# Fourteen full-precision products as pairs of fp32r products, and the order of the query stage, in a two-layer decoder step

## The chip, the cores and the metric

One core of a Trainium2 chip runs the whole step as one program. The metric is the device time of one execution in microseconds (us). The kernel before took 736.26 us (median of 3 runs, 736.24 to 736.81). 0.2% of it is 1.5 us.

## What is computed

A step of a decoder trunk with two layers, for 256 prompt tokens and 8 new tokens of running sequences; the kernel treats the 264 together, as columns of matrices whose rows are features. Cut to what matters here:

```python
def rmsnorm(x, g):
    y = xf * rsqrt(mean(xf * xf, axis=-1) + EPS)      # over the features of a token
    return y * g

# layer 0: norm, gated token MLP, residual; norm "ffn0", SwiGLU, residual
# keys:    c, kr = latent and rotary part of rmsnorm(h) @ w_dkv; c normed ("lat"), kr through rope
# layer 1: norm "mix1"; cq = rmsnorm(hn @ w_dq)  ("q"); q = cq @ w_uq   (16 heads x (128 + 64))
#          q_rope = rope(q_rope); attention over latents; residual; norm "ffn1", SwiGLU, residual
# final norm

def rope(x, pos):
    x1, x2 = split(x, 2, axis=-1)
    return concatenate([x1 * cos - x2 * sin, x2 * cos + x1 * sin], axis=-1)
```

All inputs and outputs are fp32.

## The kernel before

**Products.** A weight product in fp32 quality is made of three fp32r products (fp32r is the reduced form of fp32 that TensorE takes at a higher rate): each operand is split into a rounded high part and the rest, and `passes` (L1371) adds high by high, high by low and low by high in PSUM. The moving operand always has 264 columns (T), the stationary one is a 128x128 block. Weights come in slabs of eight blocks (512 KB): SyncE issues the load, ScalarE (ACT) rounds (`whi`, L480), GpSimd subtracts (`wlo`, L414), TensorE (PE) uses them; four slabs are in flight. Activations are rounded by ACT and subtracted by VectorE (DVE, `lo_of`, L836).

**Norm sums.** Per norm, ACT squares a tile of h (L485), DVE adds it to `acc`, which lies in PSUM bank 5; the last addition writes `total` in SBUF (L851). `norm_sum` (L1394) multiplies a 128x128 matrix of ones by `total` in plain fp32 into bank 4, after the first chunk of the next stage. ACT takes the reciprocal root (`root`), DVE refines it in three steps (`inverse_root`). Eight norms: mix0, v, ffn0, mix1, q, lat, ffn1, final.

**Rope.** Rows of two heads' rotary parts lie in 128 partitions. Their halves are exchanged by a product with a permutation matrix `swap`. DVE multiplies the query rows by sine (`tt`) and by cosine (`sq`), PE exchanges the sine part in plain fp32 (`query_swap`, L1611), DVE adds the cosine part in PSUM (`query_turned`). ACT rounds the result into `qrb` (`turned_queries`), DVE writes its low part beside it (`query_turned_low`). The rotary keys go the same way, once, through bank 5 (L1632).

**The stage "qa"** is the place of most of the change. Eight pairs of heads; per pair three chunks of nine products: chunk 0 into bank 0 (rotary parts), chunks 1 and 2 into banks 1 and 2 (the heads' other parts). Every engine works through an order written out by hand, with semaphores between them. There is one bank for each of the three chunks, so a chunk of pair p+1 can start only when DVE has read that of pair p: bank 0 when sine and cosine products are done (`rope_cos`, L1590), banks 1 and 2 when the heads' low parts are done (`qlow_done`). Turned queries lie in bank 3 (even pairs) and bank 5 (odd pairs). Bank 5 is also that of the turned keys: the first odd exchange waits for their low part (`krlo_done`, L1616).

```python
            queries(1)                         # PE, L1633
            for p in range(2, PAIRS, 2):
                query_swap(p - 2)
                query_swap(p - 1)
                queries(p)
                queries(p + 1)
```

So two exchanges stand together ahead of two pairs of chunks. DVE does two pairs per turn as well: it adds both turned queries, then takes the next pair's sine and cosine, low parts of turned queries and of heads in alternation. ACT rounds the heads (L722, L723), splits slabs between them (L480), and does the turned queries of two pairs together ahead of them. An activation table is loaded behind the queries of pair 1 (L492). The latents are scaled on DVE in pairs 2 and 3 and copied wide on ACT (L740, L743) in pairs 4 and 5. After the stage come the keys of the first pair, the sample queries (L1720) and the first scores (L1680).

Of the kernel before, what the change touches and what calls it, by code (L numbers as in the profile page):

```python
# [89 lines left out]
def build(nc, xT, w_stream, w_uv, gains, v_gain, lat_gain, q_gain, wsT, ws00_in, bs, cosT, sinT, w_ukT, pages, table,  # L90
          y_out, c_out, kr_out, v_out):
    with ExitStack() as ctx:
# [16 lines left out]
        ones = sb("ones", [P, P])  # L109
# [69 lines left out]
        swap = work[:, 6, 0:P]  # L179
# [34 lines left out]
        def room(p, n):  # L214
# [34 lines left out]
            sem, ("sq_done", "acc_done", "sum_done", "root_done", "norm_step", "rms_ready"))  # L249
        xhi_done, xlo_done = map(sem, ("xhi_done", "xlo_done"))  # L250
# [9 lines left out]
        swap_done, cqr_done, lat_done, cqs_done, cqhi_done, cqlo_done, krs_done, krsin_done, krswap_done, krsum_done, kr_done, krhi_done, krlo_done = map(  # L260
            sem, ("swap_done", "cqr_done", "lat_done", "cqs_done", "cqhi_done", "cqlo_done", "krs_done", "krsin_done", "krswap_done", "krsum_done", "kr_done", "krhi_done",
# [4 lines left out]
        q_done, qnhi_done, qlow_done, rope_cos, rope_sin, rope_swap, qr_done, qrhi_done, qrlo_done = map(  # L266
            sem, ("q_done", "qnhi_done", "qlow_done", "rope_cos", "rope_sin", "rope_swap", "qr_done", "qrhi_done", "qrlo_done"))
# [141 lines left out]
        def _(pool):  # L409
# [15 lines left out]
            pool.memset(ones[:], 1.0).then_inc(const_done, 1)  # L425
# [26 lines left out]
            for z in range(4):  # L452
                pool.tensor_copy(swap[:, 32 * z:32 * z + 32], ident[:, 32 * (z ^ 1):32 * (z ^ 1) + 32]).then_inc(swap_done, 1)
# [19 lines left out]
        def _(act):  # L473
# [29 lines left out]
            def prepare(name, m, i=0, k=0):  # L503

                at = i * k + m if k else m
                square(NQ[name], m, h[:, at, :], i, k)
                if name != "final":
                    gained(name, at)
# [4 lines left out]
            def gained(name, at):  # L513
                act.activation(xhi[:, at, :], h[:, at, :], ACT.Copy,
                               scale=gn[:, G[name], at, :]).then_inc(xhi_done, 1)
                if name == "mix1":
# [168 lines left out]
            for d in range(KQ):  # L685
                split(s0 + d + AHEAD)
                act.wait_ge(cqr_done, d + 1)
                square(NQ["q"], d, ps[:, d, 0:T])

# [12 lines left out]
            split(s0 + 2 + AHEAD)  # L702

# [25 lines left out]
            act.wait_ge(krsum_done, 1)  # L729
            act.activation(krhi, ps[:, 5, 0:NP_], ACT.Copy).then_inc(krhi_done, 1)  # L730
            act.activation(kr[:], ps[:, 5, 0:T], ACT.Copy).then_inc(kr_done, 1)
# [53 lines left out]
            turned_queries(PAIRS - 2)  # L785
# [49 lines left out]
        def _(dve):  # L835
# [4 lines left out]
            def add_square(q, m, i=0, k=0):  # L840
# [10 lines left out]
                dve.tensor_tensor(total[:] if last else acc, acc, sq[:, m % 2, :], ALU.add).then_inc(acc_done, 1)  # L851
# [29 lines left out]
            def gained(name, m, at, i=0, k=0):  # L881
                per = 2 if name == "mix1" else 1
                for z, (gain, hi, lo) in enumerate(((name, xhi, xlo), ("kv", x2hi, x2lo))[:per]):
# [3 lines left out]
                                             op1=ALU.subtract).then_inc(xlo_done, 1)  # L887

# [189 lines left out]
            for d in range(KQ):  # L1078
                dve.wait_ge(slab_used, s0 + d + 1)
                dve.tensor_tensor(ps[:, d, 0:T], ps[:, d, 0:T], Ra[:], ALU.mult).then_inc(cqr_done, 1)  # L1080
                add_square(NQ["q"], d)

# [34 lines left out]
            dve.tensor_tensor(kp, kp, Ra, ALU.mult).then_inc(krs_done, 1)  # L1117
            dve.wait_ge(krs_done, 1)
            dve.wait_ge(cqlo_done, KQ)
            dve.tensor_tensor(Ra, kp, sinb, ALU.mult).then_inc(krsin_done, 1)  # L1120
            dve.tensor_tensor(tt[:, 0, :], kp, cosb, ALU.mult).then_inc(psum_read, KQ + 3)

            def keys_turned():

                dve.wait_ge(krswap_done, 1)
                dve.wait_ge(psum_read, QA_N)
                dve.tensor_tensor(ps[:, 5, 0:T], ps[:, 5, 0:T], tt[:, 0, :], ALU.add).then_inc(krsum_done, 1)

            def keys_turned_low():
# [3 lines left out]
                dve.wait_ge(krhi_done, 1)  # L1133
# [14 lines left out]
            def query_rope(p):  # L1148
# [11 lines left out]

            def query_turned(p):

                dve.wait_ge(rope_cos, p + 1)
                dve.wait_ge(rope_swap, p + 1)
                dve.tensor_tensor(turned_bank(p), turned_bank(p), sq[:, p % 2, :], ALU.add).then_inc(qr_done, 1)
# [11 lines left out]
            keys_turned()  # L1177
            inverse_root("lat", Rc)
            keys_turned_low()
            query_rope(1)  # L1180
            query_low(1, 0)
            query_low(1, 1)
            for g in range(1, PAIRS // 2):
                query_turned(2 * g - 2)
                query_turned(2 * g - 1)
                query_rope(2 * g)
                query_turned_low(2 * g - 2)
                query_low(2 * g, 0)
                query_turned_low(2 * g - 1)
                query_low(2 * g, 1)  # L1190
                if g == 1:
                    latents(0)
                query_rope(2 * g + 1)
# [812 lines left out]
```

## Time and profile before

| | before |
|---|---|
| median of 3 runs | 736.26 us |
| profiled execution | 736.79 us |
| its span, first to last instruction | 735.1 us |
| PE busy | 725.5 us, 99% |
| ACT busy | 408.4 us, 56% |
| DVE busy | 306.8 us, 42% |
| GpSimd (POOL) busy | 534.9 us, 73% |
| granted clock of PE, mean | 0.998 |

The page and the trace come from one execution, the profiled one; 1.7 us of it lie outside the span. Busy is the time in which an engine ran at least one instruction; PE's weight loads (PEld) run beside its products. Times in time lines count from the start of the span. The profile records a plain fp32 product as two instructions, and the ends of matmuls are modelled, so that the distance between two starts says more than a duration.

### The profile page before, as it was taken

The numbers are of one execution on the slowest core, as the hardware profiler recorded it, in microseconds if no ns is written. First come the engines' busy times: TensorE is split into PE (matmuls) and PEld (weight loads), VectorE is DVE, ScalarE is ACT, GpSimd is POOL, SyncE is SP. The second block draws the span as 40 slices with busy tenths as digits, with TensorE's granted clock in tenths as the row PEclk, the third lists the DMA queues.
The fourth block names the chain that finished last, engine by engine and source line by source line (L and its number), as shares of the span: only waits on it lengthen the run. The fifth ranks groups of instructions, "written<-read, shape, count | busy, mean of one in ns | idle before, by whom it ended". The sixth has DMA issues, their size and how long they took to land.

```text
span 735.1 us, 16687 instructions
## 1 busy us (share of the span) xinstructions
PE 725.5 (99%) x6255; PEld 709.1 (96%) x6255; DVE 306.8 (42%) x777; ACT 408.4 (56%) x743; POOL 534.9 (73%) x252
## 2 busy tenths in 40 slices
PE   9999999999999999999999999999999999999995
PEld 8999999999999999999999888799999999999995
DVE  5446986233333222232488766753233333221002
ACT  7877555455444444555677576665554444444542
POOL 4895778869878888889868122149878878888891
PEclk9999999999999999999999999999999999999999
DMA  7864455656777755566576898326546555556641
GB/s 260 260 207 139 134 169 176 201 173 211 241 238 231 235 186 173 199 200 203 174 255 192 263 386 310 134 68 218 174 148 198 183 186 180 191 171 197 203 146 60
DMA packets 44842, 144.68 MB, mean 197 GB/s; under 512 B 5650, under 2 KB 6674, under 8 KB 44530
## 3 DMA queue, kind: packets, MB, share of 16 engines
q1 hardware_dynamic: 44498, 143.50, 59.3%
q8 instruction: 36, 0.59, 0.3%
q0 software_dynamic: 144, 0.40, 0.1%
q14 instruction: 20, 0.16, 0.1%
q10 hardware_dynamic: 144, 0.02, 0.0%
HBM read 142.42 MB, written 1.48 MB: 196 GB/s over the span
## 4 chain that ended last, share of the span: by engine, by line
PE 95%; DVE 2%; ACT 1%; DMA 1%; issue 0%; SPq 0%; DVEq 0%; ACTq 0%
PE ps L1373 29%; PE ps L1374 29%; PE ps L1375 29%; PE ps L1774 1%; PE ps L1750 1%; PE ps L1694 1%; DMA h<-xT 1%; PE ps L1503 1%; PE ps L1621 0%; PE ps L1754 0%; PE ps L1412 0%; PE ps L1680 0%; ACT whi L480 0%; DVE ps L851 0%; PE ps L1682 0%
## 5 line engine op out<-in xcount | busy, mean ns | idle before, releaser
L414 POOL TENSOR_TENSOR wlo<-raw,whi 128x1024 fp32r<-128x1024 f32 x221 | 527.1, 2409 | 182.5 <-ACT whi L480 182.4
L1373 PE MATMUL ps<-xhi,whi 128*128 128x264 f32 x1000 | 286.9, 287 | 0.0
L1374 PE MATMUL ps<-xlo,whi 128*128 128x264 f32 x1000 | 283.3, 283 | 0.0
L1375 PE MATMUL ps<-xhi,wlo 128*128 128x264 f32 x1000 | 283.2, 283 | 0.0
L480 ACT ACTIVATE whi<-raw 128x1024 fp32r<-128x1024 f32 x221 | 232.7, 1054 | 50.5 <-PE ps L1375 48.3
L1374 PEld LDWEIGHTS ps<-xlo,whi 128*128 128x128 f32 x1000 | 188.5, 189 | 0.2
L1373 PEld LDWEIGHTS ps<-xhi,whi 128*128 128x128 f32 x1000 | 188.3, 188 | 0.3
L1375 PEld LDWEIGHTS ps<-xhi,wlo 128*128 128x128 f32 x1000 | 187.6, 188 | 0.0
L1373 PE MATMUL ps<-ahi,whi 128*128 128x264 f32 x352 | 100.0, 284 | 0.0
L1375 PE MATMUL ps<-ahi,wlo 128*128 128x264 f32 x352 | 99.9, 284 | 0.0
L1374 PE MATMUL ps<-alo,whi 128*128 128x264 f32 x352 | 99.9, 284 | 0.0
L1035 DVE TENSOR_TENSOR h<-ps,h 128x264 f32<-128x264 f32 x31 | 13.4, 433 | 142.3 <-PE ps L1375 142.3
L1375 PEld LDWEIGHTS ps<-ahi,wlo 128*128 128x128 f32 x352 | 66.3, 188 | 0.0
L1374 PEld LDWEIGHTS ps<-alo,whi 128*128 128x128 f32 x352 | 66.2, 188 | 0.0
L1373 PEld LDWEIGHTS ps<-ahi,whi 128*128 128x128 f32 x352 | 66.2, 188 | 0.0
L664 ACT ACTIVATE ahi<-ps 128x264 f32 (+1 forms) x44 | 17.2, 392 | 87.2 <-DVE ps L1054 87.2
L1051 DVE TENSOR_TENSOR ps<-ps,work 128x264 f32<-128x264 f32 x44 | 19.4, 442 | 104.4 <-PE ps L1375 104.4
L485 ACT ACTIVATE sq<-h 128x264 f32<-128x264 f32 x39 | 16.3, 423 | 51.8 <-DVE h L1035 51.4
L661 ACT ACTIVATE sq<-ps 128x264 f32<-128x264 f32 x44 | 17.2, 392 | 41.2 <-DVE ps L1049 41.2
L1373 PE MATMUL ps<-ohi,whi 128*128 128x264 f32 x128 | 36.5, 285 | 0.0
L1373 PE MATMUL ps<-ghi,whi 128*128 128x264 f32 x128 | 36.4, 284 | 0.0
L1374 PE MATMUL ps<-glo,whi 128*128 128x264 f32 x128 | 36.3, 283 | 0.0
(266 smaller groups left out, 1148.8 us busy)
## 6 DMA issues: line engine op xcount, KB each, us to landing
raw<-w_stream SPq DMA_DIRECT2D x221, 512.0 KB, 3.4
pg<-pages SPq DMA_DIRECT2D x64, 288.0 KB, 4.5
pg<-w_ukT SPq DMA_DIRECT2D x1, 2048.0 KB, 9.3
pg<-w_uv SPq DMA_DIRECT2D x1, 2048.0 KB, 10.0
h<-xT SPq DMA_DIRECT2D x4, 264.0 KB, 4.7
raw<-w_stream SPq DMA_DIRECT2D x4, 256.0 KB, 5.5
y_out<-raw SPq DMA_DIRECT2D x4, 198.0 KB, 2.3
wsraw<-wsT SPq DMA_DIRECT2D x1, 512.0 KB, 5.6
```

Of the source, the lines that this page charges most:

```text
L414: pool.tensor_tensor(wlo[:, c % RING, :], raw[:, c % RING, :], whi[:, c % RING, :].bitcast(F32), ALU.subtract).then_inc(lo_ready, 1)
L480: act.activation(whi[:, c % RING, :], raw[:, c % RING, :], ACT.Copy).then_inc(hi_ready, 1)
L485: act.activation(sq[:, m % 2, :], src, ACT.Square).then_inc(sq_done, 1)
L661: act.activation(sq[:, w % 2, :], ps[:, (n0 + 2 * w) % BANKS, 0:T], ACT.Silu).then_inc(silu_done, 1)
L664: act.activation(ahi[:, i * 2 + w, :], ps[:, (n0 + 2 * w + 1) % BANKS, 0:T], ACT.Copy).then_inc(ahi_done, 1)
L1035: dve.tensor_tensor(h[:, at, :], ps[:, bank, 0:T], h[:, at, :], ALU.add).then_inc(psum_read, 1)
L1051: dve.tensor_tensor(up, up, Ra[:], ALU.mult).then_inc(usc_done, 1)
L1373: pe.matmul(out, whi_, mhi, start=start, stop=False)
L1374: pe.matmul(out, whi_, mlo, start=False, stop=False)
L1375: return pe.matmul(out, wlo_, mhi, start=False, stop=stop)
L1503: pe.matmul(both, vthi[:, at, c, :], wsboth[:, c, g], start=True, stop=False)
L1694: last = pe.transpose(ps[:, 2 + e, b * P:b * P + P], pr[:, e, b * P:b * P + P], ident[:])
```

## The change

1. Sums: for ffn0, mix1, q, lat and ffn1 the last addition stays in `acc` (PSUM). ACT writes its rounded part `total_hi`, DVE the rest `total_lo`, and `norm_sum` is two fp32r products with the same ones. mix0, v and final stay as they were.
2. Exchanges: rows are rounded and exchanged first, and multiplied by the sine afterwards. ACT writes `rhi` from bank 0, DVE the cosine product and the rest `rlo`; PE exchanges both in fp32r (`swap_r`); DVE multiplies by sine in place and subtracts from the cosine part. Bank 0 is free after `rlo` and the cosine product. The keys go the same way (`kphi`, `kplo`).
3. Order: PE does the exchange of pair p-1 behind chunk 0 of pair p. DVE and ACT go pair by pair. The two ACT copies of the turned keys move between the heads of pair 1. On DVE the low part of a head that frees a bank stands ahead of the low parts of turned queries, and the steps of the lat root and the low part of the keys come behind the rope products of pair 1 and the first turned queries.

```diff
+            def total_high(name):                                   # ACT
+                q = NQ[name]
+                act.wait_ge(acc_done, ACC0[q] + NORMS[q][2])
+                act.wait_ge(sum_done, q)
+                act.activation(total_hi[:], acc, ACT.Copy).then_inc(total_hi_done, 1)
...
             def queries(p, done):                                   # ACT
+                wait_query(act, 3 * p)
+                if p > 1:
+                    act.wait_ge(rope_swap, p - 1)
+                act.activation(rhi[:, p % 2, :], ps[:, 0, 0:T], ACT.Copy).then_inc(rope_hi, 1)
                 for e in range(2):
                     x = 3 * p + 1 + e
+                    if e and p == 1:
+                        act.wait_ge(krsum_done, 1)
+                        act.activation(krhi, ps[:, 5, 0:NP_], ACT.Copy).then_inc(krhi_done, 1)
+                        act.activation(kr[:], ps[:, 5, 0:T], ACT.Copy).then_inc(kr_done, 1)
...
             done = queries(1, done)
             table(ACT.Exp)
-            for g in range(1, PAIRS // 2):
-                turned_queries(2 * g - 2)
-                turned_queries(2 * g - 1)
-                done = queries(2 * g, done)
-                if g == 2:
+            turned_queries(0)
+            for p in range(2, PAIRS):
+                done = queries(p, done)
+                turned_queries(p - 1)
+                if p == 4:
                     act.wait_ge(c_done, KL)
                     act.activation(cThi[:], ps[:, 6:8, 0:NP_], ACT.Copy).then_inc(cthi_done, 1)
-                done = queries(2 * g + 1, done)
-                if g == 2:
+                if p == 5:
                     act.activation(cT[:], ps[:, 6:8, 0:T], ACT.Copy).then_inc(ct_done, 1)
...
+            def total_low(name):                                    # DVE
...
+                lo_of(total_lo[:], acc, total_hi[:]).then_inc(total_lo_done, 1)
...
-                dve.tensor_tensor(tt[:, 1 + p % 2, :], ps[:, 0, 0:T], sinb, ALU.mult).then_inc(rope_sin, 1)
+                dve.wait_ge(rope_hi, p + 1)
                 dve.tensor_tensor(sq[:, p % 2, :], ps[:, 0, 0:T], cosb, ALU.mult).then_inc(rope_cos, 1)
+                lo_of(rlo[:, p % 2, :], ps[:, 0, 0:T], rhi[:, p % 2, :]).then_inc(rope_lo, 1)
...
-            keys_turned()
-            inverse_root("lat", Rc)
-            keys_turned_low()
-            query_rope(1)
-            query_low(1, 0)
-            query_low(1, 1)
-            for g in range(1, PAIRS // 2):
-                query_turned(2 * g - 2)
-                query_turned(2 * g - 1)
-                query_rope(2 * g)
-                query_turned_low(2 * g - 2)
-                query_low(2 * g, 0)
-                query_turned_low(2 * g - 1)
-                query_low(2 * g, 1)
...
+            for p in range(1, PAIRS):
+                query_rope(p)
+                if p == 1:
+                    keys_turned()
+                query_sine(p - 1)
+                query_low(p, 0)
+                query_turned(p - 1)
+                if p == 1:
+                    inverse_root("lat", Rc)
+                    keys_turned_low()
+                query_low(p, 1)
+                query_turned_low(p - 1)
+                if p in (2, 3):
+                    latents(p - 2)
...
-            for p in (PAIRS - 2, PAIRS - 1):
-                query_turned(p)
-            query_turned_low(PAIRS - 2)
+            query_sine(PAIRS - 1)
+            query_turned(PAIRS - 1)
...
+                n = SPLIT_SUMS.index(name) + 1                      # PE, norm_sum
+                pe.wait_ge(total_hi_done, n)
+                pe.matmul(ps[:, 4, 0:T], ones_r[:], total_hi[:], start=True, stop=False)
+                pe.wait_ge(total_lo_done, n)
+                pe.matmul(ps[:, 4, 0:T], ones_r[:], total_lo[:], start=False, stop=True).then_inc(sum_done, 1)
...
-                pe.matmul(turned_bank(p), swap, tt[:, 1 + p % 2, :], start=True, stop=True).then_inc(rope_swap, 1)
+                pe.matmul(turned_bank(p), swap_r[:], rhi[:, p % 2, :], start=True, stop=False)
+                pe.matmul(turned_bank(p), swap_r[:], rlo[:, p % 2, :], start=False, stop=True).then_inc(rope_swap, 1)

             def queries(p):
                 for z in range(3):
                     query_chunk(p, z)
+                    if p and z == 0:
+                        query_swap(p - 1)
```

The exchange of pair 1 still waits for `krlo_done`. `total_high` stands on ACT right behind the last xhi of a stage (for q and lat behind the last square, and for lat behind a split), `total_low` on DVE behind the last xlo.

## Rows read from the trace of the kernel before

**Rows 1.** The page: busy us, share of the span, instructions.

```profile
PE 725.5 (99%) x6255; PEld 709.1 (96%) x6255; DVE 306.8 (42%) x777; ACT 408.4 (56%) x743; POOL 534.9 (73%) x252
```

**Rows 2.** The page: the chain that ended last, by engine.

```profile
PE 95%; DVE 2%; ACT 1%; DMA 1%; issue 0%; SPq 0%; DVEq 0%; ACTq 0%
```

**Rows 3.** Groups by form, PE: form and count, then busy us, mean ns, idle us.

```profile
L1374 PEld LDWEIGHTS ps<-xlo,whi 128*128 128x128 f32 x1000 | 188.5, 189 | 0.2
...
L1621 PE MATMUL ps<-tt,work 128*128 128x264 f32 x16 | 4.2, 386 | 0.0
...
L1399 PE MATMUL ps<-work,ones 128*128 128x264 f32 x12 | 3.6, 384 | 0.0
```

**Rows 4.** Time line, PE, at the lat sum: start us, us, what.

```profile
373.40 0.61 PE L1399 MATMUL ps<-work,ones 128*128 128x264 f32 x2
373.85 0.61 PE L1632 MATMUL ps<-work 128*128 128x264 f32 x2
...
374.42 0.28 PE L1374 MATMUL ps<-xlo,whi 128*128 128x264 f32 x1
```

**Rows 5.** Time line, PE, exchanges of pairs 0 and 1, and chunk 2.0.

```profile
377.56 1.05 PE L1621 MATMUL ps<-tt,work 128*128 128x264 f32 x4
...
378.57 0.28 PE L1374 MATMUL ps<-xlo,whi 128*128 128x264 f32 x1
...
379.66 0.28 PE L1374 MATMUL ps<-xlo,whi 128*128 128x264 f32 x1
```

**Rows 6.** Time line, ACT, stage "qa".

```profile
377.01 1.06 ACT L480 ACTIVATE whi<-raw 128x1024 fp32r<-128x1024 f32 x1
...
378.02 0.41 ACT L723 ACTIVATE ohi<-ps 128x264 fp32r<-128x264 f32 x1
378.44 1.28 ACT L492 ACT_TABLE_LOAD   x1
...
379.84 0.16 ACT L712 ACTIVATE work<-ps 128x8 f32<-128x8 f32 x1
...
380.70 0.18 ACT L712 ACTIVATE work<-ps 128x8 f32<-128x8 f32 x1
...
390.76 0.60 ACT L740 ACTIVATE cThi<-ps 128x512 fp32r<-128x512 f32 x1
```

**Rows 7.** Time line, DVE, stage "qa"; brackets: idle before, and who ended it.

```profile
375.93 0.43 DVE L867 SCALAR_TENSOR_TENSOR work<-ps,work 128x264 f32<-128x264 f32 x1
376.40 0.42 DVE L838 TENSOR_TENSOR krboth<-ps,krboth 128x256 fp32r<-128x256 f32 x1
376.74 0.42 DVE L1154 TENSOR_TENSOR tt<-ps,work 128x264 f32<-128x264 f32 x1
...
378.46 0.43 DVE L838 TENSOR_TENSOR olo<-ps,ohi 128x264 fp32r<-128x264 f32 x1 [0.61 <-ACT ohi L723]
...
379.74 0.43 DVE L1154 TENSOR_TENSOR tt<-ps,work 128x264 f32<-128x264 f32 x1 [0.16 <-PE ps L1375]
...
382.52 0.88 DVE L838 TENSOR_TENSOR qrb<-ps,qrb 64x256 fp32r<-64x256 f32 x2
383.43 0.43 DVE L838 TENSOR_TENSOR olo<-ps,ohi 128x264 fp32r<-128x264 f32 x1
383.78 0.49 DVE L1139 SCALAR_TENSOR_TENSOR ps<-ps,gl,work 128x264 f32<-128x264 f32 x1
```

**Rows 8.** Time line, PE and DVE, from the stage's end to the first scores.

```profile
402.32 1.91 PE L1720 MATMUL ps<-pg,qns 128*8 128x256 f32 x32
404.17 0.39 PE L1680 MATMUL ps<-xhi,ohi 128*128 128x256 f32 x1
...
403.14 0.69 DVE L838 TENSOR_TENSOR xhi<-ps,xhi 128x512 fp32r<-128x512 f32 x1
```

**Rows 9.** Time line, DVE and PE, around the mix1 sum.

```profile
352.98 0.43 DVE L851 TENSOR_TENSOR work<-ps,sq 128x264 f32<-128x264 f32 x1 [0.49 <-ACT sq L485]
...
354.75 0.61 PE L1399 MATMUL ps<-work,ones 128*128 128x264 f32 x2
```

More of the change, by code:

```diff
@@ L178, in build @@
         krhi, krlo = krboth[:, 0], krboth[:, 1]
-        swap = work[:, 6, 0:P]
+        swap_r = sb("swap_r", [P, P], F32R)
+        rhi, rlo = xhi[:, 4:6, :], xlo[:, 4:6, :]
+        kphi, kplo = xhi[:, 6, :], xlo[:, 6, :]
+        total_hi = sb("total_hi", [P, T], F32R)
+        total_lo = sb("total_lo", [P, T], F32R)
+        SPLIT_SUMS = ("ffn0", "mix1", "q", "lat", "ffn1")
         halves = lambda x: x.rearrange("p (a k) -> p a k", a=2)
@@ L702, in _ @@
             split(s0 + 2 + AHEAD)
+            total_high("lat")
+            act.wait_ge(krs_done, 1)
+            act.activation(kphi, ps[:, 3, 0:T], ACT.Copy).then_inc(krhi_done, 1)
             def splits_up_to(c, done):
@@ L850, in add_square @@
                     wait(dve, sum_done, q)
-                dve.tensor_tensor(total[:] if last else acc, acc, sq[:, m % 2, :], ALU.add).then_inc(acc_done, 1)
+                whole = last and not any(q == NQ[name] for name in SPLIT_SUMS)
+                dve.tensor_tensor(total[:] if whole else acc, acc, sq[:, m % 2, :], ALU.add).then_inc(acc_done, 1)
+            def total_low(name):
+                q = NQ[name]
+                dve.wait_ge(acc_done, ACC0[q] + NORMS[q][2])
+                dve.wait_ge(total_hi_done, SPLIT_SUMS.index(name) + 1)
+                dve.wait_ge(sum_done, q)
+                lo_of(total_lo[:], acc, total_hi[:]).then_inc(total_lo_done, 1)
             def inverse_root(name, R):
@@ L887, in gained @@
                                              op1=ALU.subtract).then_inc(xlo_done, 1)
+                    if z == 0 and m == KD - 1 and name in SPLIT_SUMS:
+                        total_low(name)
             dve.memset(ps[:, 5:8, T:512], 0.0).then_inc(zero_done, 1)
@@ L1398, in norm_sum @@
                 pe.wait_ge(acc_done, ACC0[q] + NORMS[q][2])
-                pe.matmul(ps[:, 4, 0:T], ones[:], total[:], start=True, stop=True).then_inc(sum_done, 1)
+                if name not in SPLIT_SUMS:
+                    pe.matmul(ps[:, 4, 0:T], ones, total[:], start=True, stop=True).then_inc(sum_done, 1)
+                    return
+                n = SPLIT_SUMS.index(name) + 1
[3 more added lines that the diff above has]
+                pe.matmul(ps[:, 4, 0:T], ones_r[:], total_lo[:], start=False, stop=True).then_inc(sum_done, 1)
             x_of = lambda b: (xhi[:, b, :], xlo[:, b, :])
@@ L1417, in busy @@
                 for _ in range(times):
-                    pe.matmul(ps[:, 3, 0:P], ones[:], ones[:], start=True, stop=True)
+                    pe.matmul(ps[:, 3, 0:P], ones, ones, start=True, stop=True)
             pe.wait_ge(const_done, 1)
@@ L1512, in _ @@
             pe.wait_ge(acc_done, ACC0[q] + KS)
-            pe.matmul(ps[:, 4, 0:NS], ones[:], total[:, NP_:T], start=True, stop=True)
+            pe.matmul(ps[:, 4, 0:NS], ones, total[:, NP_:T], start=True, stop=True)
             for c in range(2):
@@ L1611, in query_swap @@
             def query_swap(p):
-                pe.wait_ge(rope_sin, p + 1)
+                pe.wait_ge(rope_hi, p + 1)
+                pe.wait_ge(rope_lo, p + 1)
+                pe.wait_ge(swap_done, 4)
                 if p == 0:
@@ L1629, in _ @@
             norm_sum("lat")
-            pe.wait_ge(krsin_done, 1)
-            pe.wait_ge(swap_done, 4)
-            pe.matmul(ps[:, 5, 0:T], swap, Ra, start=True, stop=True).then_inc(krswap_done, 1)
-            queries(1)
-            for p in range(2, PAIRS, 2):
-                query_swap(p - 2)
-                query_swap(p - 1)
+            pe.wait_ge(krhi_done, 1)
+            pe.wait_ge(psum_read, QA_N)
+            pe.matmul(ps[:, 5, 0:T], swap_r[:], kphi, start=True, stop=False)
+            pe.matmul(ps[:, 5, 0:T], swap_r[:], kplo, start=False, stop=True).then_inc(krswap_done, 1)
+            for p in range(1, PAIRS):
                 queries(p)
-                queries(p + 1)
-            query_swap(PAIRS - 2)
             query_swap(PAIRS - 1)
@@ L1907, in _ @@
             for z in range(2):
-                pe.matmul(ps[:, SUM_BANKS[z], half[z]], ones[:], total[:, half[z]], start=True, stop=False)
+                pe.matmul(ps[:, SUM_BANKS[z], half[z]], ones, total[:, half[z]], start=True, stop=False)
             for z in range(2):
                 pe.wait_ge(sql_done, z + 1)
-                pe.matmul(ps[:, SUM_BANKS[z], half[z]], ones[:], sq[:, (KD - 1) % 2, half[z]], start=False,
+                pe.matmul(ps[:, SUM_BANKS[z], half[z]], ones, sq[:, (KD - 1) % 2, half[z]], start=False,
                           stop=True).then_inc(suml_done, 1)
```

61 lines of the change are left out of this document (32 added, 29 removed).

## The prediction

> **What bounds the kernel now.** I read the busy shares first: TensorE (PE) is busy for 99% of the span [rows 1]. The chain of work that ended last agrees: 95% of it is PE, and no other engine or queue has more than 2% [rows 2]. So PE time taken out of any stage comes off the end, as long as nobody makes PE wait in its place. The groups by form then show what the change aims at: a full-precision fp32 product is recorded as two passes, twelve for the six 264-column norm sums and sixteen for the eight query exchanges [rows 3]. Last I read the time lines of the stage "qa" (the queries), since there the change also re-orders ACT and DVE. One caution: this trace shows PE as busy whenever a modelled matmul end reaches the next start, so a wait of some tenths does not appear as idle time; start-to-start times are what to read.
>
> **What the products save.** From the start of a norm sum to the next fp32 product is 0.45 us (373.40 to 373.85). The key exchange then ends one product before 374.42: at 374.30, again 0.45 us [rows 4]. Two query exchanges run from 377.56 to 378.45 (one product before 378.57), 0.445 each. A nine-product chunk of queries runs from 378.57 to 379.66, 1.09 us or 0.121 us per fp32r product [rows 5]. Two fp32r products cost 0.24 us, so each replaced product saves 0.205 us. Eight query exchanges, one key exchange and five sums are fourteen: 2.9 us less PE work. No row shows an fp32r product right beside one of another form; bounds: 1.9 us if one of each two costs its operand's load (0.19 us [rows 3]) instead of 0.12, 3.0 us if the replaced product is taken at 0.45 and rounded up. I take 2.9, since the same fp32r form with 264 columns runs 0.121 us apart throughout [rows 5].
>
> The Trainium skill ("FP8 and Floating Point Precision", its list of precision modes) counts true fp32 as four passes, high by high down to low by low. The trace has two records per product and 0.445 against 0.121 us, 3.7 times; with four passes' worth the gain would be 14 x (4 - 2) x 0.121 = 3.4 us, an estimate by that page. The measured 0.205 stands.
>
> **The five sums.** Each gets one ACT copy (0.3 to 0.4 us) and one DVE subtraction (0.43) ahead of it, after the last addition of squares. PE works a whole chunk between the two. The tightest is mix1: the addition begins at 352.98 and ends at 353.41, the sum starts at 354.75 [rows 9]. Copy and subtraction are done by about 354.4, and the low product comes 0.12 us after the high one; the rows of xlo that PE needs earlier are written ahead of both. For "q" ACT has a split of a slab (0.95) put behind the new copy, and GpSimd has that slab to split only several us before PE wants it. Cost nothing, bounds 0 to 0.3 us each if a split slips; I take 0. POOL's and SP's queues are not changed; POOL waits longer for cT, below.
>
> **The stage of the queries.** Here the cover must be worked out. Names: chunk p.0 is the nine products of pair p's rotary queries into bank 0, p.1 and p.2 those of its heads. Before, PE needed for bank 0 only two DVE products (sine, cosine), with no ACT work ahead. Now ACT must first round (rhi), then DVE does cosine and low part: bank 0 hangs on ACT's queue. Per pair PE drops to 3 x 1.09 + 0.24 = 3.5 us, while ACT gets about 0.3 more and DVE one product more. The step times that I use, start to start: DVE product 0.34 (376.40 to 376.74), 0.47 when it waits for the one before (375.93 to 376.40), the two low halves of turned queries 0.91 (382.52 to 383.43), one latent 0.4 (0.49 long, less the tenth by which the others overlap); PE's end to DVE or ACT 0.2 (from 379.54, one product before 379.66, to 379.74); ACT's start to a DVE subtraction of its result 0.44 (378.02 to 378.46) [rows 5 to 7]. On ACT a split and the small copy behind it take 1.0 (377.01 to 378.02), ohi and table load up to the turned queries' first copy 1.82 (378.02 to 379.84), turned queries 0.86 (379.84 to 380.70), rhi or any other copy 0.28 [rows 6]. All clock times now are those of the trace before, savings of the three sums ahead left out.
>
> Pair 1. The lat sum starts at 373.40, the key exchange follows at 373.64, chunk 1.0 at 373.88 (was 374.30). It ends 374.97; rhi 375.17; DVE cosine 375.60, low part 375.95. Then DVE goes on in its order: two products for the keys (376.29, 376.76), sine 0 (377.10), a head's low part (377.45), turned 0 (377.8), three steps of the lat root (378.1, 378.6, 379.1), and only then the keys' low half, 379.55 to 380.0. PE has chunks 1.0 to 1.2 and 2.0 done at 378.46 and stands at the exchange of pair 1, whose bank 5 the keys' low half must free: **wait 1.5 us**. In the kernel before, the low half was at 376.40, ahead of all queries of pair 1.
>
> Independently, ACT is late: split 376.83, two key copies until 378.34, ohi 378.41, table load, turned 0 at 380.23, rhi 2 at 381.09; DVE has the low halves of turned 0 until 381.63, cosine 381.63, low part done at 382.46. Chunk 3.0 would come at 380.9 without the wait above and comes at 382.43 with it: the same 1.5 us again, and not in addition. So two chains bind here.
>
> Pair 3 and on. ACT from 381.09: copy, heads and two splits (0.28 + 0.17 wait + 2 x 1.3), turned 1 at 384.1, rhi 3 at 384.97. DVE: low halves of turned 1 from 384.6, latent, so cosine 3 at 385.9 and low part done at 386.75; PE is there at 385.95: **wait 0.8**. The same recurrence, with a split behind the second head of pairs 3 and 4, the wide copies of cT (0.6 us [rows 6]) ahead of rhi 5 and rhi 6, and the wide low part ahead of pair 7's cosine, gives 0.2 at chunk 5.0, 0.5 at 6.0, 0.2 at 7.0, 0.3 at the last exchange. At the hand-over, DVE takes low halves 6, sine 7 and turned 7 before the first keys' low part (0.7 us, formerly begun at 403.14): done at 406.0, PE there at 405.55 after keys and the sample queries, which took 1.85 us (402.32 to 404.17) [rows 8]: **wait 0.45**. POOL gets cT three us later than before, and has the first keys' slab split still before PE comes to it.
>
> Sum of waits: 1.5 + 0 + 0.8 + 0.2 + 0.5 + 0.2 + 0.3 + 0.5 = 4.0 us. Bounds: 1.0 us if ACT and DVE catch up wherever chains do not bind twice, 6 us if each of eight stops also costs a tenth or two of restart. Net +1.1 us. In the profiled execution: 736.8 (span 735.1 and 1.7 around it) becomes 737.9; its time is 0.5 above the median of the runs, so on the median 736.26 becomes 737.3 us.
>
> For the table load the Trainium skill ("ScalarE: Activation LUTs", What ACT_TABLE_LOAD costs) gives about 1.28 us and as much again of drain, 2.66 in all. The trace shows 1.28 and the next ACT instruction at once: 1.40 us from 378.44 to 379.84 [rows 6]. With the page's drain rhi 2 would come 1.3 us later and the sum would be +2.4; the row decides.
>
> **Rivals.** (A) Forecast, 0.48: PE's saved time is given back in waits in "qa", 736.3 to 738.3. (B) The covers hold, 0.13: waits of 0.5 us in all; 736.3 - 2.9 + 0.5 = 733.9. For it speaks that ACT and DVE have idle time in the stage; against it that ACT's work from the first split of pair 1 up to rhi 3 has only 0.2 us of idle time in my count. (C) Only the keys' low half waits, 0.15: 2.9 saved, 1.5 given back, 734.9. For it: it is the longest wait and comes from DVE's written order alone; against: the later loop needs ACT to gain 0.3 us per pair. (D) Slower, 0.24: the restart. When PE has stood, the load of the stationary operand (0.19 us [rows 3]) and the semaphore are no longer hidden behind running products; eight stops at 0.2 add 1.6: 738.9. It decides from about 0.06 us per stop on; for it speaks that rows show such a load under every product, against it that loads might go ahead of the wait.
>
> **How the numbers follow.** 0.2% is 1.5 us, what a measurement can tell here; so faster means under 734.8, slower over 737.7. Faster: B and a third of C, 0.17. Slower: D and a fifth of A, 0.33. Same: 0.50. The likeliest is A, 737.3 us, its own range 736.3 to 738.3. The range takes in C and most of D: 734.8 to 739.0; B is what is left out.
>
> **What would show it.** After: sums and exchanges 0.24 us from start to start; PE's start at the exchange of pair 1 some 1.5 us behind the end of chunk 2.0; ACT without gaps between pairs 1 and 4; rhi later than 0.2 us behind the end of chunk p.0 from pair 2 on; first scores about 1.8 us later, counted from chunk 0.0. I am wrong if the turned keys' low half is done before chunk 2.0 ends, or if chunk 4.0 follows 3.2 without a gap.

## The result, and the profile after

| | before | changed |
|---|---|---|
| median | 736.25 us | 737.57 us (737.25 to 738.03) |
| ratio, 95% interval | | 1.0019 (1.0012 to 1.0026) |
| profiled execution | 736.79 us | 737.78 us |
| its span | 735.1 us | 736.0 us |

The changed kernel is 1.3 us slower (0.9 to 1.9 by the interval), against 1.1 forecast. Each median is of 16 executions; one of those before took 1838 us, which does not move the median. The mean granted clock of PE is 0.998 in both profiled executions. The page of the changed kernel, busy us by engine and then the chain that ended last, answers to [rows 1, 2]:

```profile
PE 724.4 (98%) x6255; PEld 708.2 (96%) x6255; DVE 311.0 (42%) x791; ACT 413.1 (56%) x757; POOL 534.4 (73%) x252
...
PE 90%; DVE 5%; ACT 3%; issue 1%; DMA 1%; SPq 0%; DVEq 0%; ACTq 0%
```

PE has less work, and its share of the chain fell from 95% to 90%; DVE and ACT, 2% and 1% before, have 5% and 3%. The groups by form of the changed kernel (busy us, mean ns, idle us before) answer to [rows 3]:

```profile
L1668 PE MATMUL ps<-xhi,swap_r 128*128 128x264 f32 x8 | 2.4, 304 | 1.7 <-DVE krboth L862 1.6
L1669 PE MATMUL ps<-xlo,swap_r 128*128 128x264 f32 x8 | 2.3, 284 | 0.0
...
L1441 PE MATMUL ps<-total_hi,ones 128*128 128x264 f32 x5 | 1.4, 285 | 0.0
L1443 PE MATMUL ps<-total_lo,ones 128*128 128x264 f32 x5 | 1.4, 283 | 0.0
```

The new products are there: two fp32r products in place of each fp32 one (the profile calls the memory of `rhi` and `rlo` xhi and xlo). Whom PE waited for, by line, in the changed kernel (us in total, times, longest):

```profile
PE ps L1668 <- DVE krboth L862: 1.6, 1, 1.6
PE ps L1462 <- POOL one L434: 1.1, 1, 1.1
PE ps L1410 <- DVE xlo L862: 1.0, 2, 0.6
...
PE ps L1726 <- DVE xhi L862: 0.3, 1, 0.3
```

The wait for POOL's `one` was there before, in the first microseconds. The three rows for DVE are new, and all their waits lie between the lat sum and the first scores. PE's time line there (start us, us, what), answering to [rows 4, 5, 8]:

```profile
372.58 0.29 PE L1441 MATMUL ps<-total_hi,ones 128*128 128x264 f32 x1
372.70 0.28 PE L1443 MATMUL ps<-total_lo,ones 128*128 128x264 f32 x1
372.83 0.29 PE L1682 MATMUL ps<-xhi,swap_r 128*128 128x264 f32 x1
...
373.07 0.29 PE L1410 MATMUL ps<-xhi,whi 128*128 128x264 f32 x1
...
377.55 0.28 PE L1412 MATMUL ps<-xhi,wlo 128*128 128x264 f32 x1
379.46 0.36 PE L1668 MATMUL ps<-xhi,swap_r 128*128 128x264 f32 x1 [1.64 <-DVE krboth L862]
379.66 0.28 PE L1669 MATMUL ps<-xlo,swap_r 128*128 128x264 f32 x1
...
386.24 0.39 PE L1410 MATMUL ps<-xhi,whi 128*128 128x264 f32 x1 [0.60 <-DVE xlo L862]
386.47 0.29 PE L1411 MATMUL ps<-xlo,whi 128*128 128x264 f32 x1
...
405.69 0.36 PE L1726 MATMUL ps<-xhi,ohi 128*128 128x256 f32 x1 [0.32 <-DVE xhi L862]
```

Sum and key exchange take 0.24 to 0.25 us each (372.58 to 372.83 to 373.07). After chunk 2.0 PE stands from 377.67 (one product after 377.55) to 379.46. Who holds it is seen on DVE's time line of the changed kernel:

```profile
378.31 0.43 DVE L900 SCALAR_TENSOR_TENSOR work<-ps,work 128x264 f32<-128x264 f32 x1
378.78 0.42 DVE L862 TENSOR_TENSOR krboth<-ps,krboth 128x256 fp32r<-128x256 f32 x1
...
384.11 0.87 DVE L862 TENSOR_TENSOR qrb<-ps,qrb 64x256 fp32r<-64x256 f32 x2 [0.82 <-ACT qrb L736]
385.02 0.50 DVE L1178 SCALAR_TENSOR_TENSOR ps<-ps,gl,work 128x264 f32<-128x264 f32 x1
...
385.77 0.42 DVE L862 TENSOR_TENSOR xlo<-ps,xhi 128x264 fp32r<-128x264 f32 x1
```

The keys' low half (krboth) is written behind the root's last step and ends at 379.20. For chunk 4.0 PE waits until the low part of pair 3 ends at 386.19; that is late because DVE stood 0.82 us for ACT's turned queries, which stand behind two splits. ACT's time line of the changed kernel:

```profile
378.02 1.28 ACT L500 ACT_TABLE_LOAD   x1
...
379.42 0.16 ACT L733 ACTIVATE work<-ps 128x8 f32<-128x8 f32 x1
379.48 0.77 ACT L736 ACTIVATE qrb<-ps 64x256 fp32r<-64x256 f32 x2
...
382.70 1.08 ACT L488 ACTIVATE whi<-raw 128x1024 fp32r<-128x1024 f32 x1
...
383.70 0.79 ACT L736 ACTIVATE qrb<-ps 64x256 fp32r<-64x256 f32 x2
384.51 0.39 ACT L743 ACTIVATE xhi<-ps 128x264 fp32r<-128x264 f32 x1
```

The executions differ at their start, ahead of every edit, by up to 1.4 us (the first norm's sum starts at 16.91 us in e3 and at 18.28 us in e1), and a little at their end, so I compare stages, by PE's starts: from the lat sum to the first scores, and from there to the second half of the final norm's sum. The first norm's sum is at 17.52 us before and at 17.26 in the changed kernel. All in us; the last column is the median's distance from the kernel before, from the ratio.

| kernel | lat sum | scores | stage | rest | against before |
|---|---|---|---|---|---|
| before | 373.40 | 404.17 | 30.77 | 322.77 | |
| changed | 372.58 | 405.69 | 33.11 | 322.78 | +1.4 |
| e1_sums_only | 373.53 | 404.07 | 30.54 | 322.59 | -1.3 |
| e10_exchanges_only | 372.75 | 406.41 | 33.66 | 322.98 | +2.7 |
| e2_keys_first | 372.73 | 404.72 | 31.99 | 322.79 | +0.5 |
| e3_table_late | 372.67 | 405.78 | 33.11 | 322.78 | +1.7 |
| e4_both | 372.56 | 403.77 | 31.21 | 322.77 | -0.4 |
| e5_splits_alone | 372.75 | 404.81 | 32.06 | 322.78 | +0.4 |
| e6_splits | 373.58 | 404.96 | 31.38 | 322.78 | -0.3 |
| e7_between | 372.44 | 404.53 | 32.09 | 322.78 | 0.0 |
| e8_best | 372.63 | 404.40 | 31.77 | 323.69 | +1.0 |
| e9_ordered | 373.49 | 403.30 | 29.81 | 324.81 | +0.4 |
| e11_ordered_splits | 372.26 | 402.15 | 29.89 | 322.75 | -1.8 |
| e12_second_order | 372.58 | 401.57 | 28.99 | 322.80 | -2.4 |

The stage lost 2.34 us though ten of the fourteen replaced products lie in it.

### The profile page after: what moved, and what is told of

It reads as the page before. It is cut to its first block, busy times and chain, and to the rows that moved or that the text cites. A ratio compares the mean times of both kernels' runs of the same rounds, so it can differ in the third digit from the quotient of the medians.

```text
span 736.0 us, 16754 instructions
## 1 busy us (share of the span) xinstructions
PE 724.4 (98%) x6255; PEld 708.2 (96%) x6255; DVE 311.0 (42%) x791; ACT 413.1 (56%) x757; POOL 534.4 (73%) x252
## 4 chain that ended last, share of the span: by engine, by line
PE 90%; DVE 5%; ACT 3%; issue 1%; DMA 1%; SPq 0%; DVEq 0%; ACTq 0%
PE ps L1410 28%; PE ps L1411 28%; PE ps L1412 27%; PE ps L1820 1%; PE ps L1796 1%; DMA h<-xT 1%; PE ps L1740 1%; ACT whi L488 1%; PE ps L1547 1%; PE ps L1456 0%; DVE qrb L862 0%; PE ps L1800 0%; ACT tt L783 0%; PE ps L1726 0%; DVE ps L876 0%
```

## The experiments

My theory: the products save what was computed (0.205 us each), the sums cost nothing, and all that is lost is waits in the stage of the queries, from two chains: DVE's order (keys' low half late) and ACT's queue (table load, splits ahead of `rhi`). Rivals: the sums hide a cost; only one of the chains binds; restarts are what costs.

**e1_sums_only.** The sums as changed, exchanges and orders as before. Against the kernel before:

```diff
+        SPLIT_SUMS = ("ffn0", "mix1", "q", "lat", "ffn1")
...
+                pe.matmul(ps[:, 4, 0:T], ones_r[:], total_hi[:], start=True, stop=False)
...
+                pe.matmul(ps[:, 4, 0:T], ones_r[:], total_lo[:], start=False, stop=True).then_inc(sum_done, 1)
```

> The kernel before with the five sums alone as pairs of fp32r products; exchanges and order as before. Theory (products are worth 0.205 us each and ACT and DVE have room around the sums): 5 x 0.205 = 1.0 us less than before, 735.2 us; sums 0.24 us from start to start, no wait of PE at any of them. Rival (the copies ahead of the sums make PE wait, or a saved product is given back elsewhere): no change, or slower than before.

Measured: 735.09 us, 0.9982 (0.9972 to 0.9991): -1.3 us where five times 0.205 is 1.0. The stage is 0.23 shorter, one sum's worth, and so is the rest (0.18). So the sums' copies cost nothing that shows here.

**e10_exchanges_only.** The other half of the change: the changed kernel with plain fp32 sums.

```diff
-        SPLIT_SUMS = ("ffn0", "mix1", "q", "lat", "ffn1")
+        SPLIT_SUMS = ()
```

> The changed kernel with the five sums as plain fp32 products again. Theory (the sums' saving adds to whatever the query stage does): 1.0 us more than the changed kernel, 738.6 us; same waits of PE in the stage of the queries. Rival (the sums' copies ahead of that stage push ACT late and cause part of the waits): less than 0.5 us more, or even less time than the changed kernel.

Measured: 738.88 us, 1.0036 (1.0022 to 1.0049), 1.3 us above the changed kernel by the ratios. With e1 this splits the change: the sums bring 1.3, exchanges and order cost 2.7, together +1.4, which is the change. The same waits were expected, and they are not quite the same: the stage is 0.55 us longer than in the changed kernel where the lat sum accounts for 0.2. The other 0.35 is at chunk 6.0, where PE loses 1.04 us from start to start instead of 0.70. Why was not tried.

**e2_keys_first.** The keys' chain alone: ACT rounds the turned keys ahead of pair 1's first head, DVE adds them ahead of pair 1 and takes their low half before the head's.

```diff
-                    if e and p == 1:
+                    if e == 0 and p == 1:                       # ACT: krhi, kr
...
+            keys_turned()                                       # DVE
             for p in range(1, PAIRS):
                 query_rope(p)
                 query_sine(p - 1)
+                if p == 1:
+                    keys_turned_low()                           # was behind inverse_root
```

> The changed kernel, with the turned keys and their low half ahead on DVE (turned keys before pair 1, low half right behind sine 0) and the two key copies on ACT ahead of the heads of pair 1. Theory (two chains bind at the same place, the second is ACT's: two key copies, table load, turned queries 0, then rhi 2): the wait at the exchange of pair 1 (1.87 us lost in the changed kernel) goes, but chunk 3.0 then waits about 1 us for rhi 2, and only what ACT gained by its key copies standing earlier stays: 0.5 to 0.6 us less than the changed kernel. Rival (the keys' low half alone costs the time): 1.9 us less.

Measured: 736.78 us, 1.0007 (0.9998 to 1.0016), 0.9 under the changed kernel, where theory had 0.5 to 0.6 and the rival 1.9. Whom PE waited for in e2_keys_first:

```profile
PE ps L1410 <- DVE xlo L862: 1.5, 3, 0.8
```

and where, on its time line:

```profile
381.21 0.39 PE L1410 MATMUL ps<-xhi,whi 128*128 128x264 f32 x1 [0.82 <-DVE xlo L862]
```

The wait at the exchange of pair 1 is gone, and 0.82 us stand at chunk 3.0, where there was none: the second chain, as the theory has it. From start to start it is 1.08 us where 1.87 stood. Much of the difference is that ACT's table load came 0.56 earlier, counted from the lat sum (377.61 - 372.73 against 378.02 - 372.58), with the key copies moved. Chunk 4.0 lost 0.3 less as well (0.58 against 0.87).

**e3_table_late, e4_both.** The table load moved behind the stage, alone and together with e2's edit.

```diff
             done = queries(1, done)
-            table(ACT.Exp)
...
             act.activation(qlt[:, 0:2, :], key_views(6), ACT.Copy).then_inc(qla_done, 1)
+            table(ACT.Exp)
```

> The changed kernel with the table load for Exp taken out of the queries' stage and put behind the copy of the sample queries, where ACT waits for PE anyway. Theory (the exchange of pair 1 binds first and ACT then waits for chunk 2.1): same as the changed kernel within 0.3 us, with 1.3 us more idle time on ACT ahead of rhi 2. Rival (ACT's queue alone sets the stage): 1.4 us less.

> Both edits, keys first and table load late. Theory (both chains had to go): 1.8 us less than the changed kernel, 735.8 us, more than the sum of the two alone (0.5 and 0); the wait at the exchange of pair 1 is gone, that at chunk 3.0 is some 0.3 us, and those at chunks 4.0 and later stay. Rival (effects add up): 0.6 us less.

Measured: e3 738.3 us, 1.0023 (1.0014 to 1.0033), no gain; e4 735.9 us, 0.9995 (0.9986 to 1.0004), 1.8 under the changed kernel. PE in e3_table_late:

```profile
379.55 0.36 PE L1668 MATMUL ps<-xhi,swap_r 128*128 128x264 f32 x1 [1.63 <-DVE krboth L862]
```

and in e4_both:

```profile
380.48 0.39 PE L1410 MATMUL ps<-xhi,whi 128*128 128x264 f32 x1 [0.24 <-DVE xlo L862]
```

1.3 us of ACT work taken out brings nothing while the keys' chain holds PE. Of the stage, e3 takes 0.0, e2 1.1 and both 1.9: two chains side by side.

**e5_splits_alone, e6_splits.** A slab's split comes right behind `rhi` instead of behind a head (one split of pair 4 stays behind its first head), so that turned queries and the next `rhi` don't wait for it; e5 on the changed kernel, e6 on e4.

```diff
                 act.activation(rhi[:, p % 2, :], ps[:, 0, 0:T], ACT.Copy).then_inc(rope_hi, 1)
+                done = splits_up_to(min(QA_S + KQ * (3 * p + 1) // BLK + AHEAD + 1, PR_S + AHEAD), done)
                 for e in range(2):
...
-                    done = splits_up_to(min(QA_S + KQ * x // BLK + AHEAD + 1, PR_S + AHEAD), done)
```

> The changed kernel with one edit on ACT: the slabs' splits stand right behind rhi, ahead of the heads, instead of behind each head (one of pair 4 behind its first head). Same work, same queues otherwise. Theory (from chunk 4.0 on bank 0 is late because rhi stands behind a split and the turned queries): the 1.87 us at the exchange of pair 1 stay, those at chunks 4.0, 5.0, 6.0 (0.87, 0.09, 0.70) go for the most part: 1.3 to 1.7 us less than the changed kernel, 736.1 us. Rival (DVE's own order is what makes chunks 4.0 and 6.0 late): within 0.3 us of the changed kernel.

> All three edits: keys first, table load late, splits behind rhi. Theory: left of the waits are those of the last exchange and the hand-over (0.3 and 0.4 us) and some tenths; 1.2 us less than with the first two edits alone, 734.7 us. Rival: an earlier split makes PE wait for a weight slab or GpSimd late; no gain over the first two edits.

Measured: e5 736.89 us, 1.0005 (0.9996 to 1.0014), 1.0 under the changed kernel and short of what I expected. From start to start, the waits at chunks 4.0 and 5.0 are gone and that at 6.0 is 0.4 shorter, but those at 7.0 and the last exchange are 0.16 longer each. e6 736.18 us, 0.9996 (0.9987 to 1.0005): nothing beyond e4, where 1.2 us were expected. PE in e6_splits:

```profile
381.97 0.39 PE L1412 MATMUL ps<-xhi,whi 128*128 128x264 f32 x1 [0.36 <-DVE xlo L864]
```

Measured from start to start as in the table of the waits below, chunks 4.0, 5.0 and 6.0 lose 0.7 us less than in e4, but chunk 2.2, which lost nothing, now loses 0.36, and chunk 3.0 (this line, 0.63 against 0.51), chunk 7.0 and the last exchange lose 0.4 more together. Moving one piece in ACT's queue moved the waits.

**e7_between.** On e6: turned queries taken between the heads of the next pair, on ACT and on DVE.

```diff
                 for e in range(2):
+                    if e and p:
+                        turned_queries(p - 1)                   # ACT
...
-                query_low(p, 0)                                 # DVE
                 query_turned(p - 1)
+                query_low(p, 0)
...
-                query_low(p, 1)
                 query_turned_low(p - 1)
+                query_low(p, 1)
```

> As the run with the three edits, and the turned queries of pair p-1 on ACT between the two heads of pair p, on DVE ahead of the heads' low halves. Theory (rhi then comes 0.2 us behind the end of chunk p.0 in every pair): 0.2 to 0.5 us less than the three edits, every chunk p.0 follows without a gap. Rival (the second head becomes late and chunk p.2 waits in its place): same or slower than the three edits.

Measured: 736.63 us, 1.0000 (0.9991 to 1.0009); the rival named the place. PE's wait in e7_between:

```profile
380.02 0.39 PE L1412 MATMUL ps<-xhi,whi 128*128 128x264 f32 x1 [1.00 <-DVE olo L864]
```

and the work that it stood for, on DVE:

```profile
378.63 0.88 DVE L864 TENSOR_TENSOR qrb<-ps,qrb 64x256 fp32r<-64x256 f32 x2
379.54 0.43 DVE L864 TENSOR_TENSOR olo<-ps,ohi 128x264 fp32r<-128x264 f32 x1
```

So the order of the low halves matters, which the changed kernel has the other way round: here 0.9 us of turned queries' low halves stand ahead of a head's low part and hold bank 2, and PE with it at chunk 2.2.

**e8_best.** On e7: the first keys' low part ahead of pair 7's sine product and addition.

```diff
+            keys_low(0)
             query_sine(PAIRS - 1)
             query_turned(PAIRS - 1)
-            keys_low(0)
```

> As the run before it, with the first keys' low half on DVE ahead of sine 7 and turned 7. Theory: the 0.36 us lost ahead of the first scores go; in all about 2.9 us minus 0.3 of waits less than the kernel before, 733.8 us, faster than both kernels. Rival: the sample queries become late behind it (their copy on DVE is delayed) and the gain is nil.

Measured: 737.4 us, 1.0013 (1.0004 to 1.0022), 1.0 above e7, where 733.8 us had been expected; the rival named the sample queries. The stage is 0.3 shorter, but the rest 0.9 longer. PE in e8_best, after the first scores:

```profile
406.94 1.06 PE L1778 MATMUL ps<-ident,work 128*128 128x128 f32 x8 [0.39 <-DVE work L1253]
```

The scores have their operand earlier, and the sample queries, which need pair 7 whole, have theirs later.

**e9_ordered, e11_ordered_splits, e12_second_order.** So many places trade with each other that single moves don't find the end. From the start-to-start times of the traces I reckoned whole orders for ACT, DVE and PE, written as lists. They keep e4's edits (keys early, table late) and put the last exchange behind the first keys. e11 has e9's orders but for two splits; e12's lists differ throughout. The edit from e9 to e11, and the start of e12's list for DVE (lo: `rlo`; low: a head's low part; tlow: turned queries' low halves; trn: their addition; inv: the root's steps; kmul, ksub, krlo: turned keys):

```diff
-   "... ohi.6.0 ohi.6.1 rhi.7 tq.5 ohi.7.0 tq.6 ohi.7.1 split.10 khi tq.7 split.11"    # ACT, e9
+   "... ohi.6.0 ohi.6.1 split.10 rhi.7 tq.5 ohi.7.0 split.11 tq.6 ohi.7.1 khi tq.7"    # ACT, e11
...
+   "mem cos.0 lo.0 low.0.0 kmul inv.1 low.0.1 ksub sine.0 inv.2 trn.0 cos.1 lo.1 inv.3 krlo low.1.0
+    low.1.1 sine.1 trn.1 cos.2 lo.2 low.2.0 tlow.0 low.2.1 tlow.1 cos.3 lo.3 sine.2 ..."  # DVE, e12
```

> All fourteen products as pairs of fp32r products, with a new order of ACT, DVE and PE in the stage of the queries, laid out from the start-to-start times of the traces so that no engine makes PE wait: rhi never behind a split and turned queries together, one split per pair between the heads, the keys' low half ahead of exchange 1, exchanges of some pairs after chunk 1 or 2, the table load behind the sample queries, the first keys' low half ahead of the last turned low halves. Same work on every engine. Theory (the change loses by the order alone): from the lat sum to the first scores 28.5 to 29.5 us (30.8 before, 33.1 in the changed kernel); 2.0 to 3.0 us faster than before, 733.3 to 734.4 us. Rival (ACT and DVE have no room for the added work in any order): 31 us or more between those marks, no faster than before.

> The ordered kernel with the last two splits of the stage moved ahead on ACT (split 10 ahead of rhi 7, split 11 behind the first head of pair 7), so that GpSimd has done its last subtraction before DVE copies the rotary queries of the samples. Theory (those four copies took 2.99 us instead of 0.97 because GpSimd's subtraction ran beside them from 404.60 to 406.98, and PE then stood 1.6 us): copies about 1.0 us, the wait of PE gone, 1.7 to 2.0 us less than the ordered kernel: 734.6 us, faster than the kernel before by 0.2 to 0.3%. Rival (the copies are long for another reason, such as the table load beside them): unchanged, 736.5 us.

> The same work in a second order (exchange 0 behind chunk 1.0, the steps of the lat root spread over pair 1, one split per pair from pair 1 on), the last split behind the last head. Theory: from the lat sum to the first scores 28.7 to 29.3 us, against 29.8 in the ordered kernel; if GpSimd's last subtraction ends before the copies, 734.2 us, else up to 2 us more. Rival (PE's waits come back elsewhere): 30 us or more between the marks.

Measured: e9 736.55 us, 1.0005 (0.9996 to 1.0014), against 733.3 to 734.4 expected. The stage came out at 29.8, 1.0 under the kernel before, but the rest is 2.0 longer. Whom PE waited for in e9_ordered:

```profile
PE ps L1821 <- DVE qsl L1381: 1.6, 1, 1.6
```

DVE and POOL in e9_ordered:

```profile
404.81 2.24 DVE L1285 COPY qsr<-work 64x64 f32<-64x64 f32 x1
407.09 0.72 DVE L1285 COPY qsr<-work 64x64 f32<-64x64 f32 x3
...
404.60 2.38 POOL L439 TENSOR_TENSOR wlo<-raw,whi 128x1024 fp32r<-128x1024 f32 x1 [0.85 <-ACT whi L506]
```

and the same lines in e11_ordered_splits:

```profile
403.66 0.97 DVE L1285 COPY qsr<-work 64x64 f32<-64x64 f32 x4
...
394.75 7.10 POOL L439 TENSOR_TENSOR wlo<-raw,whi 128x1024 fp32r<-128x1024 f32 x3
```

Of four small copies from SBUF to SBUF on DVE, 2.99 us in all, the first alone took 2.24 us. It began 0.21 us after a GpSimd subtraction and ended at 407.05, 0.07 after that one's end (406.98); the other three took 0.22 each, as all four do in e11, where the subtraction was done before. ACT's table load, the rival, also ran beside e9's copies, but in e3, e4, e6, e7, e8, e11 and e12 it does so too, and there the four take 0.96 to 0.97. e11 splits these slabs earlier on ACT, so that POOL is done at 401.85. Measured: 734.43 us, 0.9975 (0.9966 to 0.9984), the same stage (29.9) and the rest at 322.75.

e12: 733.77 us, 0.9968 (0.9956 to 0.998), 2.4 us under the kernel before and 3.8 under the changed one (six executions). In e12_second_order the profile shows no wait of PE in the stage; the whole list:

```profile
PE ps L1491 <- POOL one L452: 1.1, 1, 1.1
PE ps L1983 <- ACT sq L678: 0.3, 1, 0.3
PE ps L1920 <- ACT pg L834: 0.2, 1, 0.2
```

All three lie outside the stage and are there in the kernel before as well. Its stage is 28.99 us. With no new waits the change alone would make it 30.77 - 10 x 0.205 = 28.72, so that 0.27 are left. Products and operations are the same, and only the lists differ: the 4.1 us between its stage and the changed kernel's are order alone, with that of the table load, which now stands behind the stage.

## Why the prediction was right

**The products' saving** held: 0.24 to 0.25 us for each pair of products where 0.45 stood. e1 gives 0.2 us per sum in the stage and in the rest, and e12's stage has ten products' worth less 0.3. The bound of 1.9 us (a load shown beside each product) is excluded.

**The sums at nothing** held, by e1. Copy and subtraction for mix1 in the changed kernel (start us, us, what), answering to [rows 9]:

```profile
352.52 0.44 DVE L876 TENSOR_TENSOR ps<-ps,sq 128x264 f32<-128x264 f32 x1 [0.49 <-ACT sq L493]
...
353.61 0.42 DVE L862 TENSOR_TENSOR total_lo<-ps,total_hi 128x264 fp32r<-128x264 f32 x1
...
354.29 0.28 PE L1441 MATMUL ps<-total_hi,ones 128*128 128x264 f32 x1
```

The low part is done 0.26 us before the sum starts; the prediction had 0.35.

**The waits: the sum held, its parts did not quite.** The column "lost" is the start of the second product at a place less the start of the product before the first one, less the usual 0.24; at the first scores it is less what the same two distances were before, 0.53. "Wait" is the part of it from PE's arrival (one product, 0.12 us, after the last start) to the end of the DVE instruction that PE needs, and "restart" is the remainder.

| place | predicted | lost | wait | restart |
|---|---|---|---|---|
| exchange of pair 1 | 1.5 | 1.87 | 1.53 | 0.34 |
| chunk 3.0 | 0 | 0 | 0 | 0 |
| chunk 4.0 | 0.8 | 0.87 | 0.71 | 0.16 |
| chunk 5.0 | 0.2 | 0.09 | 0 | 0.09 |
| chunk 6.0 | 0.5 | 0.70 | 0.53 | 0.16 |
| chunk 7.0 | 0.2 | 0.22 | 0.06 | 0.16 |
| last exchange | 0.3 | 0.31 | 0.13 | 0.18 |
| first scores | 0.5 | 0.36 | 0.24 | 0.12 |
| sum | 4.0 | 4.4 | 3.2 | 1.2 |

The chain to the keys' low half was laid out step by step and ends where it was said: 6.60 us after the lat sum's start by the prediction, 6.62 in the trace. PE's own arrival too: 5.06 against 5.09. So the wait of 1.5 held to some hundredths. What was put at nothing is the way back: 0.26 us from DVE's end (379.20) to PE's start there, and a second product 0.20 after the first, not 0.12. Over the stage the waits proper are 3.2 us, 0.8 less than predicted, and the restarts, in the forecast only as a rival and in the upper bound, are 1.2. The two errors nearly cancel in the 4.4, and that is luck. With them the stage adds up: 30.77 - 10 x 0.205 + 4.4 = 33.1, and 33.11 was measured.

Of the signs named in advance, PE's start at the exchange of pair 1 is 1.79 us behind the end of chunk 2.0 (1.5 was said), and the first scores come 2.3 us later (1.8 was said). ACT is not without gaps between pairs 1 and 4: it waits for PE twice, 0.41 us ahead of 381.08 and 0.43 us ahead of 385.68.

**"So two chains bind here"** is shown by e2, e3 and e4 in this sense: the second one is as long as the first within some tenths, neither edit alone brings what both do, and the first wait is paid once. In the changed kernel itself the second one does not bind. Counted from the lat sum, the prediction had its end at 9.06 us and PE at chunk 3.0 at 9.03. In the trace its end is at 381.56 (start us, us, what):

```profile
381.14 0.42 DVE L862 TENSOR_TENSOR xlo<-ps,xhi 128x264 fp32r<-128x264 f32 x1
...
381.97 0.28 PE L1410 MATMUL ps<-xhi,whi 128*128 128x264 f32 x1
```

That is 8.98 us after the lat sum, and PE comes to chunk 3.0 at 9.39, 0.4 us later. So the table load alone, e3, could bring nothing.

**The rivals.** (B), the covers hold: no, they needed another order. e11 and e12 are what B describes, and e12 lies at 733.8 where B said 733.9. (C), only the keys' low half waits: no. With that wait taken away C leaves none, 736.3 - 2.9 = 733.4; e2 gave 736.8. (D), a restart of 0.2 us at every stop, is largely true in its mechanism: 1.2 us at seven stops, 0.17 each. That is well over the 0.06 from which the prediction says that it decides. It did not come out at D's 738.9 because the waits proper were 0.8 us shorter than in the sum that D adds to.

**The table load** has no drain in the changed kernel either: 1.40 us from its start to the next copy (378.02 to 379.42). The 1.38 us of drain that the Trainium skill ("ScalarE: Activation LUTs", What ACT_TABLE_LOAD costs) adds to the load do not show.

**What the forecast left out, and what does not add up.** The ffn1 sum's 0.2 us, which e1 has in the rest (322.59), is offset in the kernels with changed exchanges (322.75 to 322.80, e12 too; 322.98 in e10, without that sum; e8 and e9 lose more, as told above). The traces show where, 7.9 us after the first scores, at the product that turns the samples' probabilities (`sq`). Before:

```profile
411.97 0.28 PE L1375 MATMUL ps<-cThi,wlo 128*128 128x256 f32 x1
412.08 0.43 PE L1764 MATMUL ps<-ident,sq 128*128 128x128 f32 x2
```

and in the changed kernel, with the ACT instruction that writes `sq`:

```profile
413.44 0.28 PE L1412 MATMUL ps<-cThi,wlo 128*128 128x256 f32 x1
413.77 0.44 PE L1810 MATMUL ps<-ident,sq 128*128 128x128 f32 x2
...
413.15 0.47 ACT L798 ACTIVATE sq<-ps,nms 128x256 f32<-128x256 f32 x1 [0.64 <-DVE nms L1298]
```

PE starts it 0.33 us after the product before instead of 0.11. `sq` waits for DVE's `nms`, which starts 7.01 us after the first scores (412.70) instead of 6.84 (411.01). DVE works from the first keys' low part on with one gap, 0.39 us in both kernels. That part ends 0.15 us before the first scores now and 0.34 before them in the kernel before, so everything behind it is about 0.2 us later, counted from the scores. No run took this wait away, so it is read from the traces and not tried.

Counted from lat sum to the end the changed kernel loses 2.35 us, and it gains 0.56 ahead of the lat sum (372.58 against 373.40, less 0.26 by which its first norm's sum began earlier): +1.8, where the medians say +1.4 (interval 0.9 to 1.9). So by the stages the forecast of 1.1 is 0.7 short, and the medians lie nearer to it than its terms do; what makes the 0.4 between traces and medians stays open.

## What to carry to other kernels

Here PE was busy 98 to 99% of the time, and its savings were real only where the engines that free its banks came earlier by as much. Before such a change lay out, start to start, every instruction of the feeding engines for one turn, and give each stop a price for the restart beside the wait. Where two chains reach nearly the same wait, an experiment on one of them understates it (e2) or shows nothing (e3), and only both together (e4) or a new order as a whole (e12) shows what the change is worth. Look at what comes right behind the stage as well: e8 and e9 won in it and gave it back a few microseconds later.

## What the runs showed of the hardware

- A GpSimd subtraction of 128x1024 did not slow DVE's copies from SBUF to SBUF: the one copy that began beside it took until it was over (2.24 us instead of 0.22, ending 0.07 us after it, e9), and the next ones took their usual 0.22. The subtraction took 2.38 us, its usual length (7.10 for three in e11). In the changed kernel DVE's `xlo` from `h` and `xhi`, all in SBUF, behaves alike: 0.49 us alone, up to 2.73 beside a GpSimd subtraction. DVE's low parts read from PSUM (`olo`, 128x264) took 0.42 us with and without one.
- A stop of PE costs more than the wait. At the chunks of the changed kernel it is 0.05 to 0.06 us from DVE's end to PE's start (386.19 to 386.24 at chunk 4.0) and a second product 0.11 late, 0.16 us in all. At the last exchange it is 0.18 and at the exchange of pair 1 0.34, with 0.26 us from DVE's end to PE's start. The chunks have two waits written ahead of their first product, the last exchange four and that of pair 1 five; whether that is why was not tried.
